# Recurrence inputs of an RWKV layer: another order of the six products of a unit, and the last unit's gate and bonus finished one stage later

## The reference

```python
r, k, v = einsum('nbsd,nde->nbse', xm[:3], w_rkv)
decay = exp(-exp(-softplus(-(w0 + tanh(xw @ w1) @ w2)) - 0.5))
a = sigmoid(a0 + (xa @ a1) @ a2)
g = sigmoid(xg @ g1) @ g2
kk = k * k_k;  kk = kk / max(sqrt(sum(kk * kk over the head)), 1e-12)
k = k * (1 + (a - 1) * k_a)
state recurrence over (r, decay, k, v, -kk, kk * a) gives y
y = groupnorm(y) * lnx_g + lnx_b
y = (y + sum(r * k * r_k over the head) * v) * g
```

## Time and profile before

| | before |
|---|---|
| median of 3 executions | 3757.14 us (3756.17 to 3758.62) |
| the profiled execution | 3752.29 us |
| its span in the trace | 3750.5 us |
| PE busy | 3538.6 us, 94% |
| DVE busy | 2294.0 us, 61% |
| `rwkv_inputs`, loop over the units on PE | 2122.30 to 2334.81 us |
| first matmul of `rwkv_chunks` | 2346.57 us |

### The profile page before, as it was taken

One profiled execution on the slowest core, in us unless ns is written; L12 is line 12 of the kernel. 1 busy time (PEld: TensorE's weight loads), 2 busy tenths in 40 slices (PEclk: granted clock), 3 DMA queues, 4 the chain that ended last, 5 costly groups with the idle time before them and its releaser, 6 DMA issues. The chain is left out here.

```text
span 3750.5 us, 58365 instructions
## 1 busy us (share of the span) xinstructions
PE 3538.6 (94%) x22109; PEld 2871.8 (77%) x22109; DVE 2294.0 (61%) x3621; ACT 1483.8 (40%) x2442; POOL 1345.3 (36%) x822
## 2 busy tenths in 40 slices
PE   8999988998998999899999899898999998989998
PEld 4787866788988999788888343887888864677887
DVE  5713167416999887788888766445566236646642
ACT  3212255324445996333333243223255314424540
POOL 3724300424876334544222011330243521413352
PEclk9999988999999999999999999999899997699999
DMA  7634310625777899999999254203333331033331
GB/s 283 223 96 134 139 48 19 230 96 186 229 226 270 322 324 354 358 368 365 356 352 341 66 152 135 73 32 117 89 89 100 113 131 46 1 130 85 96 117 57
DMA packets 367108, 651.14 MB, mean 174 GB/s; under 512 B 23944, under 2 KB 227592, under 8 KB 363716
## 3 DMA queue, kind: packets, MB, share of 16 engines
q1 hardware_dynamic: 320028, 472.96, 38.0%
q0 software_dynamic: 36864, 134.23, 9.6%
q10 hardware_dynamic: 10024, 41.29, 2.8%
HBM read 557.64 MB, written 96.00 MB: 174 GB/s over the span
## 5 line engine op out<-in xcount | busy, mean ns | idle before, releaser
L97 PE MATMUL ex_hb<-wb_x_hi,ex_uh 128*128 128x384 f32 x1024 | 350.5, 342 | 22.7 <-POOL ex_ul L1677 22.7
L2404 POOL TENSOR_TENSOR pf_wl<-pf_raw,pf_wh 128x2048 fp32r<-128x2048 f32 x48 | 222.4, 4635 | 388.4 <-ACT pf_wh L2333 388.4
L98 PE MATMUL ex_hb<-wb_x_lo,ex_uh 128*128 128x384 f32 x1024 | 344.5, 336 | 0.0
L99 PE MATMUL ex_hb<-wb_x_hi,ex_ul 128*128 128x384 f32 x1024 | 344.3, 336 | 0.0
L97 PE MATMUL es_ob<-es_vh,es_ah 128*128 128x512 f32 x768 | 300.3, 391 | 10.7 <-DVE es_al L2046 10.7
L97 PE MATMUL pf_acc<-wb_x_hi,pf_wh 128*128 128x512 f32 (+2 forms) x768 | 298.2, 388 | 6.9 <-DVE wb_x_lo L2451 4.7
L98 PE MATMUL es_ob<-es_vl,es_ah 128*128 128x512 f32 x768 | 299.9, 391 | 0.0
L99 PE MATMUL es_ob<-es_vh,es_al 128*128 128x512 f32 x768 | 299.7, 390 | 0.0
L98 PE MATMUL pf_acc<-wb_x_lo,pf_wh 128*128 128x512 f32 (+2 forms) x768 | 297.6, 388 | 0.0
L99 PE MATMUL pf_acc<-wb_x_hi,pf_wl 128*128 128x512 f32 (+2 forms) x768 | 297.6, 387 | 0.0
L2025 POOL DMA_INDIRECT es_near<-in_peer_v,wb_picked x128 | 178.3, 1393 | 325.8 <-DVE wb_po L2049 319.7
(11 more groups left out here) (516 smaller groups left out, 8869.8 us busy)
## 6 DMA issues: line engine op xcount, KB each, us to landing
ex_u<-in_uT SPq DMA_DIRECT2D x128, 512.0 KB, 4.6
es_v<-in_peer_v SPq DMA_DIRECT2D x31, 2048.0 KB, 17.1
pf_raw<-in_w_up SPq DMA_DIRECT2D x88, 512.0 KB, 5.1
ip_raw<-in_w_in SPq DMA_DIRECT2D x112, 256.0 KB, 4.1
scratch_act<-ex_ge SPq DMA_DIRECT2D x128, 192.0 KB, 4.8
scratch_G<-eg_gates ACTq DMA_DIRECT2D x12, 2048.0 KB, 9.1
es_ge<-scratch_act SPq DMA_DIRECT2D x31, 768.0 KB, 6.0
es_g<-scratch_G SPq DMA_DIRECT2D x31, 768.0 KB, 10.0
```

The source lines that it names most:

```text
L97: pe.matmul(out, left[0], right[0], start=start, stop=False)
L98: pe.matmul(out, left[0], right[1], start=False, stop=False)
L99: return pe.matmul(out, left[1], right[0], start=False, stop=stop)
L2404: pool.tensor_tensor(wl[:, u], raw[:, u], wh[:, u].bitcast(F32), ALU.subtract).then_inc(w_lo, 1)
```

## The change

- `ORDER` becomes a, decay, k, r, v, gate (4, 3, 1, 0, 2, 5), and DVE's work on a unit is put in that order: first what needs a and decay, then k, and what needs r last.
- The matmul that sums the squares stands in the middle of r's eight matmuls, not behind them. ACT takes the root before it copies r.
- POOL's three steps for unit 7 move from `rwkv_inputs` to `rwkv_chunks`, behind the level masks of the first pair, and SP stores bonus and gate of that unit there, behind the loads of units 2 and 3.
- The operands and v of unit 7 are stored as soon as their own counters allow (the fourth operand, and the copy of v), without waiting for the gate.
- Bonus, gate and norm get tiles of their own (`gates`) that outlive the stage, and `ri_work` shrinks to 28 tiles. `STORED` is 32 lower for the odd units, since two of their stores have another counter.

```diff
-    ORDER = (1, 4, 3, 0, 2, 5)
+    ORDER = (4, 3, 1, 0, 2, 5)
...
-                for u in range(2):
-                    store(KD // 2 - 1, u)
+                store(KD // 2 - 1, 0)
+                sp.wait_ge(parts_done, (KD - 1) * 5 + 5)
+                sp.dma_start(d["arbk"][KD - 1], arbk[:, 1]).then_inc(stored[1], 16)
+                sp.wait_ge(copied, (KD // 2 - 1) * 12 + 6 + AT[2] + 7)
+                sp.dma_start(d["vg"][0].rearrange("(q p) t -> p q t", p=P)[:, KD - 1, :], a5[:, 1, 2]).then_inc(stored[1], 16)
...
                                 for k in range(KD):
+                                    if what == 0 and k == KD // 2:
+                                        pe.wait_ge(squared, n + 1)
+                                        pe.wait_ge(rooted, n + 1)
+                                        pe.matmul(two[:, 0, :], ones[:], sq, start=True, stop=True).then_inc(summed, 1)
                                     mm = pe.matmul(acc[:, j, :], wt[:, u, what, k, :], xm[:, what, k, :], start=(k == 0),
...
-                            if what == 0:
-                                pe.wait_ge(squared, n + 1)
-                                pe.wait_ge(rooted, n + 1)
-                                pe.matmul(two[:, 0, :], ones[:], sq, start=True, stop=True).then_inc(summed, 1)
...
                                 act.activation(sq, a5[:, u, 1], ACT.Square, scale=cols[:, 0, q]).then_inc(squared, 1)
-                            if what == 0:
                                 act.wait_ge(summed, n + 1)
                                 act.wait_ge(nrm_used, n + 1)
                                 act.activation(nrm, two[:, 0, :], ACT.Sqrt).then_inc(rooted, 1)
...
+                        ready(0)
+                        dve.tensor_tensor(t1, r, kn, ALU.mult).then_inc(unit_steps, 1)
                         dve.wait_ge(unit_steps, n * 3 + 3)
-                        dve.tensor_tensor(arbk[:, u, 2], b, rc, ALU.mult).then_inc(parts_done, 1)
+                        dve.tensor_scalar(t1, t1, cols[:, 2, q], None, ALU.mult).then_inc(rk_done, 1)
+                        dve.tensor_tensor(arbk[:, u, 1], r, c, ALU.mult).then_inc(parts_done, 1)
...
+                with pool.Fori(0, KD // 2 - 1) as i:
                     for u in range(2):
...
+                        gated(i * 2 + u, bass.ds(i * 2 + u, 1), u)
+                gated(KD - 2, slice(KD - 2, KD - 1), 0)
...
+                last = slice((KD - 1) * P, KD * P)
+                sp.wait_ge(gate_steps, 2)
+                sp.dma_start(d["bonus"][last, :], bonus[:, 1]).then_inc(gate_stored, 16)
+                sp.wait_ge(gate_steps, 3)
+                sp.dma_start(d["vg"][1][last, :], gate[:, 1]).then_inc(gate_stored, 16)
                 for n in range(SLOTS, KD):
...
+                    if n == 0:
+                        pool.tensor_tensor(bonus[:, 1], bonus[:, 1], norm[:, 1, KD - 1:KD].to_broadcast([P, T]),
+                                           ALU.add).then_inc(gate_steps, 1)
+                        pool.wait_ge(gate_steps, 1)
+                        pool.tensor_tensor(bonus[:, 1], bonus[:, 1], gate[:, 1], ALU.mult).then_inc(gate_steps, 1)
+                        pool.wait_ge(gate_steps, 2)
+                        pool.tensor_tensor(gate[:, 1], gate[:, 1], norm[:, 0, KD - 1:KD].to_broadcast([P, T]),
+                                           ALU.mult).then_inc(gate_steps, 1)
```

More of the change, by code:

```diff
@@ L2552, in rwkv_inputs @@
         pc, ar, bk, vT, *masks = carried
-        work = sb("ri_work", [P, 32, T])
-        dx, xl = work[:, 8:16], work[:, 16:32].rearrange("p (u k) t -> p u k t", u=2)
+        bonus, gate, norm = gates
+        work = sb("ri_work", [P, 28, T])
+        dx, xl = work[:, 4:12], work[:, 12:28].rearrange("p (u k) t -> p u k t", u=2)
         a5 = work[:, 0:10].rearrange("p (u n) t -> p u n t", u=2)
@@ L2559, in rwkv_inputs @@
         arbk = work[:, 20:28].rearrange("p (u n) t -> p u n t", u=2)
-        bonus, gate = work[:, 28:30], work[:, 30:32]
         acc = ps("ri_acc", [P, 6, T])
@@ L2742, in _ @@
                         dve.wait_ge(stored[u], i * (16 * STORES) + 16 * STORES)
-                        ready(1)
-                        step(dve.tensor_scalar(kk, k, cols[:, 0, q], None, ALU.mult), wait=False)
                         ready(4)
-                        step(dve.tensor_scalar(t2, a, -1.0, cols[:, 1, q], ALU.add, ALU.mult))
-                        step(dve.scalar_tensor_tensor(kn, t2, 1.0, k, ALU.add, ALU.mult), wait=False)
+                        step(dve.tensor_scalar(t2, a, -1.0, cols[:, 1, q], ALU.add, ALU.mult), wait=False)
                         ready(3)
@@ L2751, in _ @@
                         step(dve.tensor_tensor_scan(c, b, rc, 0.0, ALU.mult, ALU.add))
-                        ready(0)
-                        dve.tensor_tensor(t1, r, kn, ALU.mult).then_inc(unit_steps, 1)
                         step(dve.reciprocal(rc, c), wait=False)
-                        dve.wait_ge(unit_steps, n * 3 + 1)
-                        dve.tensor_scalar(t1, t1, cols[:, 2, q], None, ALU.mult).then_inc(rk_done, 1)
                         step(dve.tensor_copy(cp64[:, :, 1:RC], c64[:, :, 0:RC - 1]), wait=False)
                         step(dve.tensor_copy(pc[:, q, :].rearrange("p o e -> p (o e)"), c64[:, :, RC - 1]))
-                        dve.tensor_tensor(arbk[:, u, 1], r, c, ALU.mult).then_inc(parts_done, 1)
+                        ready(1)
+                        step(dve.tensor_scalar(kk, k, cols[:, 0, q], None, ALU.mult), wait=False)
+                        step(dve.scalar_tensor_tensor(kn, t2, 1.0, k, ALU.add, ALU.mult))
                         dve.tensor_tensor(arbk[:, u, 3], kn, rc, ALU.mult).then_inc(parts_done, 1)
@@ L2781, in _, with gated, rwkv_chunks @@
             def _(pool):
+                def gated(n, q, u):
+                    pool.wait_ge(bonus_done, n + 1)
+                    pool.tensor_tensor(bonus[:, u], bonus[:, u], norm[:, 1, q].to_broadcast([P, T]), ALU.add).then_inc(bonus_steps, 1)
+                    pool.wait_ge(bonus_steps, n * 2 + 1)
+                    pool.tensor_tensor(bonus[:, u], bonus[:, u], gate[:, u], ALU.mult).then_inc(bonus_steps, 1)
+                    pool.wait_ge(bonus_steps, n * 2 + 2)
+                    pool.tensor_tensor(gate[:, u], gate[:, u], norm[:, 0, q].to_broadcast([P, T]), ALU.mult).then_inc(out_ready, 1)
                 pool.wait_ge(small_loaded, 80)
-                with pool.Fori(0, KD // 2) as i:
+                with pool.Fori(0, KD // 2 - 1) as i:
                     for u in range(2):
-                        n = i * 2 + u
-                        q = bass.ds(n, 1)
-                        pool.wait_ge(bonus_done, n + 1)
-                        pool.tensor_tensor(bonus[:, u], bonus[:, u], norm[:, 1, q].to_broadcast([P, T]), ALU.add).then_inc(bonus_steps, 1)
-                        pool.wait_ge(bonus_steps, n * 2 + 1)
-                        pool.tensor_tensor(bonus[:, u], bonus[:, u], gate[:, u], ALU.mult).then_inc(bonus_steps, 1)
-                        pool.wait_ge(bonus_steps, n * 2 + 2)
-                        pool.tensor_tensor(gate[:, u], gate[:, u], norm[:, 0, q].to_broadcast([P, T]), ALU.mult).then_inc(out_ready, 1)
-def rwkv_chunks(nc, d, gt, hs, carried, stored, slot_loaded, masks_loaded, r_all, y_all):
+                        gated(i * 2 + u, bass.ds(i * 2 + u, 1), u)
+                gated(KD - 2, slice(KD - 2, KD - 1), 0)
+def rwkv_chunks(nc, d, gt, hs, carried, gates, stored, slot_loaded, masks_loaded, r_all, y_all):
     LEVELS = 5
@@ L2807, in rwkv_chunks @@
             w_copied, d_done, x_added, mv_done, mv_copied, az_done, az_copied, rg_done, r_ready, y_ready, yh_done, g_ready,
-            h_ready), ExitStack() as ctx:
+            h_ready, gate_steps, gate_stored), ExitStack() as ctx:
         sb, ps = tensors(nc, ctx)
+        bonus, gate, norm = gates
         _, ar01, bk01, vT01, mask2, lmask, emask, eye, ident, _, _ = carried
@@ L3068, in lower @@
                     if n == 0:
-                        dve.wait_ge(stored[0], STORED)
-                        dve.wait_ge(stored[1], STORED)
+                        dve.wait_ge(stored[0], STORED[0])
+                        dve.wait_ge(stored[1], STORED[1])
                     low = pp[:, n % 2, 2:4, 0:half * RC].rearrange("p c (i t) -> p c i t", t=RC)
@@ L3163, in _ @@
                 for u in range(2):
-                    act.wait_ge(stored[u], STORED)
+                    act.wait_ge(stored[u], STORED[u])
                 for n in range(0, KD, 2):
@@ L3198, in _ @@
                 for u in range(2):
[L3199 removed]
+                    pool.wait_ge(stored[u], STORED[u])
                 for n in range(0, KD, 2):
@@ L3382, in rwkv_recurrence @@
         hs = sb("rr_hs", [P, KD, NC_, RC])
-        rwkv_chunks(nc, d, gt, hs, carried, stored, slot_loaded, masks_loaded, r, y)
+        rwkv_chunks(nc, d, gt, hs, carried, gates, stored, slot_loaded, masks_loaded, r, y)
```

(3 more changed lines are left out.)

25 lines of the change are left out of this document (13 added, 12 removed).

## The result

The changed kernel takes 3741.64 us (median of 8 executions, 3730.75 to 3745.33) against 3756.16 us (median of 8, 3751.34 to 3759.14) of the kernel before beside it: a ratio of 0.9962, with a 95% interval of 0.9952 to 0.9972. The profiled execution took 3741.73 us with a span of 3739.9, 10.6 less than the span before.

The account below looks back on a forecast made before the run. PE's own matmuls were taken to bound the loop, with PE waiting only at the stage border. Border 9.6 plus entrance 1.2 less loop 0.4 gave 10.4 us off 3757.14: 3746.7 us, range 3743 to 3752 (its own range 3744.5 to 3749.5).

Parts of the forecast that it names:

- row that was to show it right: Signs in the new profile: full PE loop, bonus within 0.2 us, gap 1.9 to 2.7, clock 1.00, first transpose after 6 us.
- The sum: Whole stage of the change: 9.6 + 1.2 - 0.4 = 10.4 us gained.
- a microsecond of scatter below: Allowance for scatter at the lower end of the forecast range, 3743 to 3752 us.
- The border: From rwkv_inputs to rwkv_chunks: PE's gap falls from 11.76 us to 2.1, a gain of 9.6 (9.1 to 9.9).
- the barrier: Last link of PE's gap between the stages: priced at 1.0 us, from 0.88 behind ACT at the next one, not 1.56.
- The entrance: First matmul to first transpose of rwkv_chunks: the clock stays 1.00, gain 1.75, taken as +1.2 (+1.75 to -0.8).
- both halves of the doubt about it: Start of rwkv_chunks: the clock may fall anyway, or instructions come late and up to 3.8 us of stall returns.
- The loop: Over the units in rwkv_inputs: no gain, as PE never waits; splitting r's group loses 0.4 us (0 to 0.8).
- POOL's steps: Three steps moved into rwkv_chunks behind the first pair's masks: cost nothing; without that cover 3.6 us would come back.
- The first: At the stage border and entrance: clock falls despite the short gap, or code comes late; about 3749.5 us; chance 0.20.
- The second: In the loop: PE waits for ACT's squares in the middle of r; up to 3765 us; chance 0.07.
- The third: At the stage border: an engine, SP or DVE, is late at the barrier; 3753.5 us; chance 0.08.

Follow-up runs that it names:

- warm with late loads: Changed kernel plus one unread matmul at the loop's end and chunk-stage loads issued behind the first pair's batches: 3737.78 us, ratio 0.9960 against the kernel before.
- steps first: Changed kernel with POOL's three steps for unit 7 ahead of its masks of the first pair: 3739.96 us, ratio 0.9962 against the kernel before.

## Why the prediction was wrong

**The mechanisms held, but for the clock at the entrance.** Nearly every other row that was to show it right is there: PE 53 of 53 us in the loop, a unit of 26.53 us, no wait of PE for ACT or DVE, the square at T + 10.5, the bonus 0.12 us behind PE's sum, t1 done at T + 22.0 where T + 22.7 was the bound. The sum was 10.4 us; the stage gave 10.4 in the mean of two and three traces, and 12.1 (10.1 to 14.2) came out over all executions. The two first traces alone differ by 12.3 in the stage, as the one of before has 1.06 us of low clock ahead of the loop (48 rows of the last low-rank group in 23.89 us instead of 22.82) and the longer stall of the earlier trace rows.

**The step that failed** is the one that turned the gain into a time: "I take the 10.4 off the median", 3757.14, with "a microsecond of scatter below". Three executions that lay within 2.5 us were taken for the kernel's time. Over 85 executions it is 3753.4 with a standard deviation of 4.8 us, and medians of eight to 27 came out between 3751.7 and 3756.2. Less 10.4, these 3753.4 give 3743.0, so 3.7 of the 5.1 us by which the forecast of 3746.7 missed lie here; the other 1.4 are within the scatter of a median of eight. The profiled execution, 3752.29, less 10.4 gives 3741.9, but one execution is that near by luck. The kernel before, run beside the changed one, came to 3756.16, itself 2.8 above its median over all, so the gain read 14.5 us. The microsecond below was worked out from nothing, where the scatter asks for several. The terms stayed in their ranges but for the border, which is 0.05 us under its bound. Their best ends give 9.9 + 1.75 = 11.65 us and 3745.5, so the 3744.5 was not their sum.

**The border** gained 9.05 us; I took 9.6, and 9.1 was the lower bound. The term that was off is the barrier. PE starts 2337.97 - 2336.07 = 1.90 us behind the end of DVE's bonus: 0.3 of hand-over and 1.6 of barrier, the 1.56 of the earlier trace rows, not the 0.88 of the earlier trace rows that I chose because a compute engine comes last. In the run with the move alone it is 1.90 us again (2337.49 - 2335.59), with DVE late. Order and move alone gave 2.4 and 6.7 of it.

**The entrance** gained 1.0, also between the means of the repeats, taken as 1.2, but not in the way I said. The prediction had the clock at 1.00 there, and that did not hold: the clock did fall, later and for a shorter time: 3.4 us at 0.50, where it was 13.7. The 6.0 us worked out for an entrance at full speed were right (5.98 in warm with late loads), and so were both halves of the doubt about it: with the clock kept up, a stall took back 0.6. The Trainium skill, "TensorE: Matmul & The Clock Gate", section "What's actually happening", says that the share of work at the lower level varies from run to run. The traces agree, above all behind the stage: 141.3 us at 0.50 in one execution of the kernel before, 183.2 in another.

**The loop** lost nothing: 211.73 against 211.92. The 0.4 us for one more border inside r were not there. (60 rows at 0.43 us are 25.8 us, not 25.7; it changes nothing.)

**POOL's steps** cost nothing, as taken. Every DVE instruction beside them, in the changed kernel and with the steps first, has an operand from PSUM and takes 1.22 us with the steps and without. The Trainium skill, "SBUF — State Buffer", section "SBUF: two separate sides", says that GpSimd and DVE lock each other out of a shared pair of ports, for DVE operations in a two-port mode or with two SBUF inputs; one with an operand from PSUM is not named. The trace agrees: line 3087, with two SBUF inputs, takes 0.68 us when it starts ahead of POOL and 1.77 behind. So the steps are free by where they stand; beside an instruction of that kind each might cost DVE up to its own 1.0 to 1.3 us, an estimate from the rows that no run has tried.

**The rivals.** The first came true in its condition (the clock fell) but not in its price. The second did not occur, and its arithmetic was too kind: it priced a wait at its own length, while in the middle of r 5.4 us of waiting cost 7.5 us of loop, and squares behind r cost 22.6 us of stage for 7.6 us of waiting (18.2 in the loop, the rest at the entrance and behind it, where stall and clock came out worse). The third did not occur.

**What stays open:** whether the change touches anything outside its stage. The 12.1 us over all executions and 10.4 in the stages don't contradict each other, but the interval leaves room for 3.8 more. And what fills PE's stalls: that they go with the loads is shown, that PE waits for its instructions behind them is only argued.

## What to carry to other kernels

Before a predicted gain is taken off a measured time, ask how far executions of equal code lie apart; three that agree don't tell. To shorten a gap at a barrier, write its chain down row by row and give each link a price from the same chain: here the gains of the two parts added up to within 0.02 us, and only the barrier's price, borrowed from another place, was off. Work that an engine does behind the last result of the bound engine can go into the next stage, wherever that engine would wait anyway, and a PE wait inside a full loop is to be priced by the clock too, not by its length alone.
